# A two-block transformer layer pair on one core: input rows loaded by channels, norms applied when tiles leave PSUM

## The reference, cut to what matters

```python
def _rmsnorm(x, w):
    y = x * rsqrt(mean(x * x, axis=-1) + EPS) * w
def first_block(x, ...):
    h = _rmsnorm(x, norm_w)
    proj = h @ w_in              # aq ak av az dq dk dv dz and 16 gate columns
    attn = neighbourhood_attention(rmsnorm(aq), rmsnorm(ak), av) * silu(az)
    dq, dk, dv = split(silu(depthwise_conv5([dq, dk, dv])))
    o = gated_delta(l2norm(dq), l2norm(dk), dv, gates)   # both directions
    delta = rmsnorm(o) * silu(dz)
    return x + concat(attn, delta) @ w_out
def second_block(x, ...):
    # stick-breaking attention (8 heads) and a chunked retention
    # with rotated queries and keys (4 heads), merged by two gates
    ...
```

## Time and profile before

| what | value |
|---|---|
| median of 3 runs | 2318.49 us (2314.53 to 2320.6) |
| the profiled execution | 2317.61 us |
| its span in the profile | 2315.8 us |
| busy TensorE / VectorE / ScalarE / GpSimd | 96% / 46% / 41% / 16% |
| mean granted clock of TensorE | 0.966 of full |

### The profile page before, as it was taken

One profiled execution on the slowest core, in us unless ns is written; L12 is line 12 of the kernel. 1 busy time (PEld: TensorE's weight loads), 2 busy tenths in 40 slices (PEclk: granted clock), 3 DMA queues, 4 the chain that ended last, 5 costly groups with the idle time before them and its releaser, 6 DMA issues.

```text
span 2315.8 us, 29173 instructions
## 1 busy us (share of the span) xinstructions
PE 2218.5 (96%) x11599; PEld 1813.5 (78%) x11599; DVE 1073.5 (46%) x2014; ACT 948.8 (41%) x1745; POOL 366.7 (16%) x603
## 2 busy tenths in 40 slices
PE   7999998889998899999999999998999999999998
PEld 6778776767788688788887788786888888888886
DVE  4344444353346443566555664655514342433441
ACT  4464644343455243555455555543313232233220
POOL 3200112362702210000000000003301211010111
PEclk9999989899698899999999999999999999999999
DMA  5522335343752332112110211112121111344232
GB/s 162 192 84 64 96 93 166 96 139 93 231 208 83 127 111 64 41 46 64 33 60 23 64 55 46 37 46 69 60 69 46 46 55 46 127 132 164 91 105 86
DMA packets 171384, 209.76 MB, mean 91 GB/s; under 512 B 36576, under 2 KB 124752, under 8 KB 169712
## 3 DMA queue, kind: packets, MB, share of 16 engines
q1 hardware_dynamic: 150752, 141.51, 19.6%
q0 software_dynamic: 20496, 66.39, 9.1%
HBM read 150.41 MB, written 53.77 MB: 88 GB/s over the span
## 4 chain that ended last, share of the span: by engine, by line
PE 86%; ACT 4%; DVE 3%; POOL 3%; DMA 2%; issue 1%; SPq 0%; POOLq 0%; DVEq 0%; ACTq 0%
PE PS L1686 12%; PE PS L1688 12%; PE PS L1687 12%; PE PS L1680 9%; PE PS L1681 9%; PE PS L1682 9%; PE PS L1652 5%; PE PS L1961 3%; PE PS L1940 3%; PE PS L1744 2%; PE PS L1770 2%; PE PS L1993 1%; PE PS L2006 1%; PE PS L1801 1%; DMA RAW<-in_w_in 1%
## 5 line engine op out<-in xcount | busy, mean ns | idle before, releaser
L1686 PE MATMUL PS<-WH,HH 128*128 128x512 f32 x1344 | 547.3, 407 | 13.4 <-DVE WK L2419 10.5
L1688 PE MATMUL PS<-WH,HL 128*128 128x512 f32 x1344 | 528.2, 393 | 0.0
L1687 PE MATMUL PS<-WH,HH 128*128 128x512 f32 x1344 | 527.4, 392 | 0.0
L1680 PE MATMUL PS<-HH,WH 128*128 128x512 f32 (+1 forms) x976 | 399.3, 409 | 3.0 <-DVE WH L2386 3.0
L1682 PE MATMUL PS<-HH,WH 128*128 128x512 f32 (+1 forms) x976 | 382.7, 392 | 0.0
L1681 PE MATMUL PS<-HL,WH 128*128 128x512 f32 (+1 forms) x976 | 382.6, 392 | 0.0
L1686 PEld LDWEIGHTS PS<-WH,HH 128*128 128x128 f32 x1344 | 255.3, 190 | 71.8 <-DVE WK L2419 12.1
L1688 PEld LDWEIGHTS PS<-WH,HL 128*128 128x128 f32 x1344 | 254.4, 189 | 55.3
L2386 DVE SCALAR_TENSOR_TENSOR WH<-RAW,WK,WH 128x512 fp32r<-128x512 f32 (+2 forms) x248 | 179.8, 747 | 246.7 <-ACT WH L2015 245.3
L1687 PEld LDWEIGHTS PS<-WH,HH 128*128 128x128 f32 x1344 | 255.6, 190 | 46.0
L2015 ACT ACTIVATE TM<-PS 128x512 f32<-128x512 f32 (+3 forms) x285 | 154.2, 556 | 324.3 <-PE PS L1688 204.1
(11 more groups left out here) (307 smaller groups left out, 2902.3 us busy)
## 6 DMA issues: line engine op xcount, KB each, us to landing
RAW<-in_w_in SPq DMA_DIRECT2D x200, 256.0 KB, 3.0
RAW<-in_w_out SPq DMA_DIRECT2D x32, 256.0 KB, 3.7
sig_d<-WK POOLq DMA_DIRECT2D x32, 256.0 KB, 2.3
WK<-sig_d POOLq DMA_DIRECT2D x32, 256.0 KB, 3.1
WK<-in_rpb POOLq DMA_DIRECT2D x16, 480.0 KB, 4.9
RAW<-in_w_in SPq DMA_DIRECT2D x32, 192.0 KB, 3.0
dnc_d<-TM SPq DMA_DIRECT2D x12, 512.0 KB, 3.5
TM<-dnc_d SPq DMA_DIRECT2D x10, 512.0 KB, 4.7
```

Source lines behind the costliest of these rows:

```text
L1680: e.matmul(ps, wh, hh, start=k == 0, stop=False)
L1686: e.matmul(ps, hh, wt[:, 0:width], start=k == 0, stop=False)
L1687: e.matmul(ps, hh, wt[:, 512:512 + width], start=False, stop=False)
L1688: mm = e.matmul(ps, hl, wt[:, 0:width], start=False, stop=k == 7)
```

## The change

- x is given a second time, transposed, as `x_t`, and loaded in eight slices of 128 channels (`x_load(k)`), each ahead of the weight slice of the same step. The constants `ident` and `norm_w` count on one semaphore, for which the first weights' copy waits; `norm_w` is now the first transfer and `ident` comes behind four slices of x and four of the weights.
- ScalarE and VectorE make the high and low parts straight from the slice (item `xc`), with no norm, no transpose and no PSUM. ScalarE squares the slice (`xq`), GpSimd adds the squares of the eight slices, and item `xs` sums them over channels by eight one-column products on TensorE, a copy on VectorE and one power on GpSimd, for all tokens at once. Item `xb` turns the factors into a row form by broadcasting transposes in PSUM bank 7, four and four, copied to the last slot of WH, which the X blocks give up: they have ten slots instead of eleven, the blocks after them eleven as before.
- The first six tiles of dz are taken together: for each k all six, in six banks (`together`). The ring has seven banks until the attention begins, instead of six. Then come `xs`, tiles 6 and 7, and the evacuations as a stream of its own (`first_out`).
- The factors are put on at the evacuations: as the scale of ScalarE's Silu (dz) and copy (na), and in dn by VectorE, which now evacuates those tiles, multiplying with the row form.
- `rc` has a cost of 5000 ns in the plan.

```diff
-NSLOT, NRAW = 11, 4
+NSLOT, XSLOT, NRAW = 11, 10, 4
...
+def slot_of(n):
+    return n % XSLOT if n < 8 * len(X) else n % NSLOT
...
+        "rc": [("dma", 5000)],
...
-    state = {"ring": list(range(6)), "n": 0, "open": None}
+    state = {"ring": list(range(7)), "n": 0, "open": None}
...
+    def together(b, tiles):
+        for t in tiles:
+            take(("tile", b, t))
+        for k in range(8):
+            there = 5500.0 + 2800.0 * k
+            put("xc", k, after=there)
+            put("w", k, after=there)
+            put("xq", k, after=there)
+        prepped[0], plan.clock["bus"] = 8, there
+        put("c1")
+        for k in range(8):
+            plan.until(plan.known["w", k])
+            for t in tiles:
+                put("g", b, t, k)
+        put("xs")
+        plan.spawn(first_out(b))
+
+    def first_out(b):
+        for t in range(8):
+            yield has("xs")
+            yield has("g", b, t, 7)
+            slot(("ev", b, t), "stg", 3)
+            put("ev", b, t)
+            plan.now[0] += 1200.0
+            if t in (1, 3):
+                yield
+                put("xb", t // 2)
+            yield
...
     for name in X:
...
-        gemm(b, x_ready if name == "dz" else None)
+        gemm(b)
         if name == "dz":
             put("dg")
...
-            x_load(0)
-            e.dma_start(ident, masks[0]).then_inc(c_const, 16)
             e.dma_start(nw, norm_w).then_inc(c_const, 16)
             for n in range(NRAW):
+                x_load(n)
                 load(n)
-            x_load(1)
+            e.dma_start(ident, masks[0]).then_inc(c_const, 16)
...
+                    if BLOCKS[b] == "dz":
+                        w.wait_ge(*at["xc", k, "lo"])
...
+                elif kind == "xs":
+                    for t in range(8):
+                        mm = e.matmul(bank(7, 1, t), chunk(xss, t), one, start=True, stop=True)
+                elif kind == "xb":
+                    for j in range(4):
+                        i = 72 + 4 * a[0] + j
+                        mm = tr(bank(7, 128, j * 128), rs[:, i:i + 1].to_broadcast([128, 128]))
...
                         i, n = slots[item]
                         w.wait_ge(c_stg[i], 16 * n)
-                        e.activation(stg[i], ps, ACT.Silu).then_inc(*w.sig(*item, "z"))
+                        w.wait_ge(*at["xs", "r"])
+                        e.activation(stg[i], ps, ACT.Silu, scale=rs[:, 72 + t:73 + t]).then_inc(*w.sig(*item, "z"))
...
+                            tt(raw(n)[:, th * 512:(th + 1) * 512], ps, scale, ALU.mult).then_inc(*w.sig(*item, "out"))
...
+                    k = a[0]
+                    if k:
+                        w.wait_ge(*at[(*item, "sq")])
+                        w.wait_ge(*w.last)
+                        e.tensor_tensor(xss, xss, xsq[k % 2], ALU.add).then_inc(*w.sig(*item, "a"))
```

More of the change, by code:

```diff
@@ L451, in bank_free @@
         if before:
+            if before[:2] == ("tile", 0):
+                plan.drain(has("ev", *before[1:]))
             if before[0] == "tile":
@@ L454, in bank_free @@
             plan.until(plan.known.get(before, 0.0))
+    def together(b, tiles):
[25 more added lines that the diff above has]
+            yield
     def gemm(b, ready=None, after=None):
         tiles = tiles_of(b)
-        for t in tiles:
+        if BLOCKS[b] == "dz":
+            together(b, tiles[:6])
+        n_slot = XSLOT if b < 9 else NSLOT
+        for t in tiles[6:] if BLOCKS[b] == "dz" else tiles:
             if ready:
@@ L468, in gemm @@
                 put("g", b, t, k)
-                if end and prepped[0] < 8 * b + 16 and prepped[0] - NSLOT < 8 * b + k + 1:
+                if end and prepped[0] < 8 * b + 16 and prepped[0] - n_slot < 8 * b + k + 1:
                     prep(True)
@@ L491, in gemm @@
                 after(t)
-            if not end and prepped[0] < 8 * b + NSLOT:
+            if not end and prepped[0] < 8 * b + n_slot:
                 prep(True)
[L497 to L508, removed]
     put("c0")
     put("dnc")
[L512 to L517, removed]
     def na_side(p):
@@ L2111, in _ @@
                             o = tokens(buf_of(b))[:, t, :]
-                        copy(o, ps).then_inc(*w.sig(*item, "out"))
+                        copy(o, ps, rs[:, 72 + t:73 + t] if name[:2] == "na" else None).then_inc(*w.sig(*item, "out"))
                 elif kind == "nq":
@@ L2409, in _ @@
                     name = BLOCKS[b]
+                    if name[:2] == "dn":
+                        c, th = t
+                        ps, scale = bank(place["tile", b, t][0]), norms[:, th * 512:(th + 1) * 512]
+                        w.wait_ge(*at["g", b, t, 7, "done"])
+                        w.wait_ge(*at["xb", th, "out"])
+                        if c == 3:
+                            for sem, v in z_stores():
+                                w.wait_ge(sem, v)
+                            tt(GT16[:, th * 512:(th + 1) * 512], ps[0:16, :], scale[0:16, :],
+                               ALU.mult).then_inc(*w.sig(*item, "out"))
+                        else:
+                            n = 3 * int(name[2]) + c
+                            if n >= 2:
+                                before = divmod(n - 2, 3)
+                                w.wait_ge(*at["cv", *before, 4, "d"])
+                                if before[1] < 2:
+                                    w.wait_ge(*at["cn", *before, "n"])
+                            else:
+                                w.wait_ge(*at["xq", 7, "sq"])
+                                w.wait_ge(*at["xc", 7, "lo"])
+                            tt(raw(n)[:, th * 512:(th + 1) * 512], ps, scale, ALU.mult).then_inc(*w.sig(*item, "out"))
                     if name[:2] == "na" or name[0] == "h":
```

138 lines of the change are left out of this document (81 added, 57 removed).

## The result

The changed kernel takes 2330.68 us, median of 5 runs (2323.49 to 2338.26), against 2318.49 for the kernel before; the ratio is 1.0053, 95% interval 1.0032 to 1.0074. It is slower by half a per cent. The forecast was 2324.5, with a range of 2306 to 2333 and its own case 2317 to 2331; it gave 0.44 to a change too small to tell from none and 0.38 to a slower kernel.

What follows compares the result with a forecast made beforehand. TensorE, 96% busy, was taken to bound the kernel. From 2317.6 us the terms -4.7 + 0.4 + 14.2 + 2.0 + 1.0 + 0 - 6.0 = +6.9 gave 2324.5, range 2306 to 2333.

Steps and rivals of the forecast that it cites:

- Start, -4.7: Start of dz: without the 64 transposes, block dn0 starts at 64.3 instead of 69.0; bounds -7.5 and -2.
- The identity's term: Kernel start: the identity lands at 14.0 behind 3.1 MB, so the first matmul comes at 15.5 against 15.15.
- the feeding: Weight steps of dz: GpSimd and VectorE by turns need 4.2 us, 0.1 more than TensorE; lead covers it, cost nothing.
- Rival C: Start: shared turns cost VectorE and GpSimd more than 4.1 us a step, dn0 after 68; 2329.5, chance 0.10.
- Stall, +14.2: Early dn0: the fill holds the fifth tile's store, so TensorE waits before the squares' column sums; bounds 0 and +17.
- P: The start of block dn0, from which the forecast counts the times of the fill, the store and the squares' sums.
- Clock after it, +2.0: After the stall: TensorE runs at half pace for 2.8 to 5.65 us, which costs half; range 1.4 to 2.8.
- Second turn and gates, +0.4 and +1.0: Inside dn0 the second turn of norms adds 0.4; VectorE, also evacuating dn, is late for the gates, 1.0 (0 to 4).
- Order, slots, recursion, 0 (-5 to +5): X blocks and recursion: another order with ten slots, TensorE's work the same; bounds two thirds of a 7.2 us wait.
- My sign for a miss: A difference over 8 us arising between 330 and 800 would show the term set to 0 as the one missed.
- Tables, -6.0: First rotation near 1600: eight more weight steps cut TensorE's wait from 9.1 to 3.6, perhaps 1.4 of half pace; -7 to 0.
- Rival B: Early dn0: the stall isn't there, store not held by the fill or conv chain covered; 2308.3, chance 0.22.

Runs made afterwards that it cites:

- experiment 3: The changed kernel with the seven additions of the squares on VectorE instead of GpSimd, the identity as late as before: 2325.0 us, ratio 1.0032.
- experiment 5: The changed kernel with the six transfers of the zero fill issued by ScalarE at the same place, off GpSimd's queue: 2328.0 us, ratio 1.0036.

## Why the prediction came out as it did

The time lies in the range and in the forecast's own case, 6.2 us over the forecast itself; the profiles show 13.1 where the sum had 6.9. That it came so near is in part luck: the start was 3.2 us worse than its term and the stall 2.0 better, and the terms from 330 us on are no larger than what two profiles of one program differ by. Point by point, against the terms:

- *Start, -4.7.* Measured -1.5, off the term and just outside its bounds (-7.5 and -2). The identity's term was nearly right: forecast first matmul 15.5, measured 16.41. The step that failed is the feeding, "2.2 + 2.0 = 4.2 us": I let one addition stand against the two VectorE operations of a step. In the trace seven additions meet seven VectorE operations. Each of these but the first takes 2.1 to 2.2 us longer, as long as I had estimated for a whole addition, and an addition takes 3.0 us on average with its own waiting: so two additions went through per step, as long as there were any. VectorE's step grew to 6.1 us, and TensorE waited for it 0.68 us at 31.76 and 1.76 at 37.88. The Trainium skill's page "SBUF — State Buffer", section "SBUF: two separate sides", says that whichever of the two starts first has the shared pair for its whole instruction; the trace agrees with that rule (3.42 us for 1.23, 2.86 for 0.75), and it was its consequence that the prediction worked out wrongly. Rival C was true in its mechanism, and the lead that I counted against it was used up after three steps; experiment 3 puts its price at 2.8 us, and its sign (dn0 after 68) was missed by half a microsecond.
- *Stall, +14.2.* Measured 12.21 of waiting, in the forecast place, on the forecast chain: fill at P+6.6 (forecast P+6.3), store landed at P+24.0 (P+25.3), squares ready 14.0 later (14.7), TensorE there at P+25.9 (P+25.8). The fill took 16.7 us and not 18.9. The evidence that I gave, the tables' wait on the same queue, is not the whole of it: in experiment 5 the store was late with the fill on another queue. The Trainium skill's page "DMA: Bandwidth & Descriptors", section "Two DMAs through the same engine are not ordered", allows a later transfer to complete first; on the fill's own queue no store here did (the changed kernel's landed 0.7 us behind the fill's last part), and from another queue it landed 0.2 us ahead of that part.
- *Clock after it, +2.0.* Matmuls at half pace (0.43 from one to the next) run from 105.57 to 112.96, 7.4 us, which costs 3.7. That is more than the upper bound of 2.8, which came from 5.65 us of half pace at the start. Removing the fill from its place brought 18 to 20 us and not 12.2 + 3.7 = 15.9; the rest lies within the intervals, and no run assigns it.
- *Second turn and gates, +0.4 and +1.0.* With the stall removed, the lag grows by 1.8 from dn0 to the gates: right.
- *Order, slots, recursion, 0 (-5 to +5).* Net +2.3 from the gates to the rotation in the trace, less than two profiles of one program differ by there; ten slots alone cost 2.3 by the ratio, with 0 in the interval. Right in sum, and by luck: it is a gain of some 15 and a loss of some 13 that nearly cancel, and the bounds, taken from one wait of 7.2, allowed for neither. My sign for a miss, a difference over 8 us that arises between 330 and 800, does not catch it if the two ends are compared (+22 and +20.4).
- *Tables, -6.0.* The wait is 3.61 as forecast, and the lag falls by 5.6. In the kernel before the edit alone brings 5.3.

Sum of the measured: -1.5 + 1.8 + 12.2 + 3.7 + 2.3 - 5.6 = 12.9, against 13.1.

Rival B gave 2308.3 with the stall gone. With the fill moved it is 2310.9, which is B and 2.6 us, near the 3.2 that the start fell short. The same change with the fill behind the stores is faster than the kernel before; what made it slower was the fill in front of four stores, and the identity behind 3 MB and GpSimd's additions kept most of the start's gain from it.

## What to carry to other kernels

When tiles are made side by side, their evacuations come in one burst: look at what now stands between the burst and the buffer that it reuses, and move bulk transfers behind it. Here, issuing the fill from another engine's queue did not help: the store beside it was late all the same, and the issuing engine lost the time of the issues. A constant that gates the first operation goes ahead of the data, however small it is. Where GpSimd and VectorE work on long operands at once, price each VectorE operation with one whole GpSimd operation, not one per step, as long as GpSimd has work queued. And before a difference of a few us between two profiles is explained, look at two profiles of one program: here they differed by up to 8.

## What the runs showed of the hardware

- Beside a 5.6 MB fill of DRAM (16.7 us in the changed kernel) transfers on every queue were slow: a 256 KB store took 12.4 us on the fill's own queue and 7.3 on another (issued 5.0 and 10.1 us after the fill's first issue), weight loads of 192 KB on a third 7.1 to 13.1 instead of about 3.
- DMA issues by ScalarE took 0.6 us each for the first two and 1.0 to 1.4 for the next four (GpSimd's same six 0.6 to 0.8); ScalarE did no other work in that time.
- While GpSimd's additions of 128x1024 followed one another, each VectorE operation with two operands in SBUF took 2.1 to 2.2 us longer (3.42 for 1.23, 2.86 for 0.75), and seven additions took 20.96 us. On VectorE the same seven took 8.5.
- After 12.2 us of idle time TensorE ran 7.4 us at 1.2 GHz (granted clock 0.50). The granted clock also falls to 0.50 near 600 in every kernel, with TensorE busy for 127 to 133 of the 140 us from 560 to 700 (mean 0.80 before, 0.70 to 0.82 in the others, which is 50 to 84 us at 0.50 in all). In one program it was 0.76 twice and 0.80 once. What sets how long it lasts is open.
